# Delta rule on one Trainium2 core: three groups of 64x64 products written as tiles of 64 rows by 32 columns

## The reference

```python
def rwkv7_scan(r, w, k, v, kk, a, S0):
    def step(S, xs):
        r_t, w_t, k_t, v_t, kk_t, a_t = xs
        sa = jnp.einsum('bhvk,bhk->bhv', S, -kk_t)
        S = (S * w_t[:, :, None, :] + sa[..., None] * (kk_t * a_t)[:, :, None, :]
             + v_t[..., None] * k_t[:, :, None, :])
        y = jnp.einsum('bhvk,bhk->bhv', S, r_t)
        return S, y
```

## Time and profile before

| | |
|---|---|
| Median of 3 runs | 2491.67 us (2488.76 to 2494.94) |
| Profiled execution | 2489.43 us, span 2487.6 us |
| TensorE busy | 2423.0 us, 97% of the span, 46610 matmul records |
| VectorE, ScalarE busy | 1280.5 us (51%), 606.9 us (24%) |
| DMA | 500.52 MB, mean 201 GB/s |
| RWKV block of layer 0 | from about 395 to 670 us |
| RWKV block of layer 1 | from about 1385 to 1656 us |

### The profile page before, as it was taken

How to read it: one execution, slowest core, us unless ns; L and a number is a source line. 1 busy time by engine, 2 the same in 40 slices (tenths; PEclk the granted TensorE clock), 3 DMA queues, 4 the chain that set the end, 5 groups by cost and what they waited for, 6 DMA issues and landing times. The chain is left out here.

```text
span 2487.6 us, 105448 instructions
## 1 busy us (share of the span) xinstructions
PE 2423.0 (97%) x46610; PEld 2013.6 (81%) x46610; DVE 1280.5 (51%) x3333; ACT 606.9 (24%) x1798; POOL 0.2 (0%) x4
## 2 busy tenths in 40 slices
PE   9999999999999999999999999999999999999998
PEld 7987666666699999898766666679899989888887
DVE  7666666666687676756665666668311111111111
ACT  2234333433311100223333334321111111111111
POOL 0000000000000000000000000000000000000000
PEclk9999999999999999999999999999999999999999
DMA  6334432222243443333343222234799999999997
GB/s 251 129 138 146 165 121 88 84 84 80 101 154 133 157 165 138 133 134 137 137 162 129 82 77 84 84 105 152 300 363 397 383 371 407 400 381 408 387 392 309
DMA packets 146068, 500.52 MB, mean 201 GB/s; under 512 B 18784, under 2 KB 23520, under 8 KB 143360
## 3 DMA queue, kind: packets, MB, share of 16 engines
q1 hardware_dynamic: 145792, 496.44, 53.5%
HBM read 476.08 MB, written 20.29 MB: 200 GB/s over the span
## 5 line engine op out<-in xcount | busy, mean ns | idle before, releaser
L302 PE MATMUL psum<-hT,ring 128*64 128x144 f32 (+1 forms) x4568 | 458.5, 346 | 3.4 <-DVE hT L2430 1.7
L455 PE MATMUL psum<-work,ring 128*64 128x88 f32 (+3 forms) x11264 | 417.6, 232 | 16.2 <-issue 5.8
L455 PEld LDWEIGHTS psum<-work,ring 128*64 128x64 f32 x11264 | 399.3, 136 | 35.4 <-issue 30.1
L302 PEld LDWEIGHTS psum<-hT,ring 128*64 128x64 f32 x4568 | 294.4, 137 | 95.0 <-issue 11.3
L2966 DVE TENSOR_TENSOR work<-psum,work 128x88 f32<-128x88 f32 (+3 forms) x176 | 42.4, 241 | 362.7 <-PE psum L455 362.5
L2667 PE MATMUL psum<-work,proj 128*64 128x88 f32 (+3 forms) x5632 | 203.5, 232 | 6.1 <-issue 4.5
L2667 PEld LDWEIGHTS psum<-work,proj 128*64 128x64 f32 x5632 | 196.8, 136 | 12.6 <-issue 9.6
L1776 ACT ACTIVATE work<-psum 128x256 f32<-128x256 f32 (+4 forms) x320 | 103.9, 362 | 349.9 <-PE psum L1687 84.8
L302 PE MATMUL psum<-work 128*64 128x144 f32 (+4 forms) x2096 | 155.4, 283 | 4.3 <-DVE work L1267 3.6
L302 PE MATMUL psum<-y_ret,work 128*64 128x144 f32 x2400 | 156.2, 286 | 0.8 <-DVE y_ret L532 0.8
L302 PEld LDWEIGHTS psum<-y_ret,work 128*64 128x64 f32 x2400 | 148.6, 137 | 1.0 <-issue 1.0
(11 more groups left out here) (518 smaller groups left out, 3695.7 us busy)
## 6 DMA issues: line engine op xcount, KB each, us to landing
ring<-w_ff_dram SPq DMA_DIRECT2D x424, 512.0 KB, 7.4
ring<-w_mix_dram SPq DMA_DIRECT2D x256, 512.0 KB, 3.8
proj<-w_ff_dram SPq DMA_DIRECT2D x128, 512.0 KB, 5.5
proj<-w_ff_dram SPq DMA_DIRECT2D x64, 384.0 KB, 5.8
work<-s_gla_dram SPq DMA_DIRECT2D x8, 1024.0 KB, 4.9
gla_s_out<-work SPq DMA_DIRECT2D x8, 1024.0 KB, 4.7
work<-s_ret_dram SPq DMA_DIRECT2D x8, 512.0 KB, 5.1
ret_s_out<-work SPq DMA_DIRECT2D x8, 512.0 KB, 2.7
```

The lines of the kernel that those rows point to most:

```text
L302: last = nc.tensor.matmul(out[64 * c:64 * c + 64], weights[:, 64 * c:64 * c + 64], x, start=start, stop=stop)
L455: mm = nc.tensor.matmul(out[64 * c:64 * c + 64], ring[:, s, k, 64 * c:64 * c + 64], rhs[:, k0 + k, :], start=(k0 + k == 0), stop=(k0 + k = ...
```

## The change

Three groups of products in the RWKV block are written with a new helper, `in_quarters`: the first product of every level (`level_w`), the product of the last level, and keys by values in `right_side`. The two halves of a pair are cut in two each, at 32 columns of the stationary operand, so that for each c four matmuls on tiles of 64 rows by 32 columns stand in place of two on 64 by 64. The order for a c is: columns 0 to 31 of both halves, then columns 32 to 63 of both. Each of the four streams all 64 columns of its half's moving operand. Results, waits and semaphores stay as they were. Operands, buffers and all other instructions too.

```diff
+            def in_quarters(outs, weights, xs):
+
+                for j in range(0, CH, 32):
+                    for r in range(2):
+                        last = mm(outs[r][j:j + 32], weights[r][:, j:j + 32], xs[r], start=True, stop=True)
+                return last
+
             def level_w(i, n):
...
                 for c in range(6 if n == 0 else 4):
-                    for r in range(2):
-                        last = mm(unit(half(W, r), c), half(AT, 1 - r)[:, c], half(X, 1 - r)[:, c], start=True, stop=True)
+                    last = in_quarters([unit(half(W, r), c) for r in range(2)], [half(AT, 1 - r)[:, c] for r in range(2)],
+                                       [half(X, 1 - r)[:, c] for r in range(2)])
                 last.then_inc(sig("W1_ps"), 1)
...
                 else:
                     for c in range(4):
-                        for r in range(2):
-                            last = mm(unit(half(W, r), 4 + c), half(W1, r)[:, c], half(XT, r)[:, c], start=True, stop=True)
+                        last = in_quarters([unit(half(W, r), 4 + c) for r in range(2)],
+                                           [half(W1, r)[:, c] for r in range(2)], [half(XT, r)[:, c] for r in range(2)])
...
                 for c in range(4):
-                    for r in range(2):
-                        mm(unit(half(W, r), c), half(PkPr, r)[:, c, 0], half(vtok, r)[:, c], start=True, stop=True)
+                    in_quarters([unit(half(W, r), c) for r in range(2)], [half(PkPr, r)[:, c, 0] for r in range(2)],
+                                [half(vtok, r)[:, c] for r in range(2)])
```

## The result

The changed kernel takes 2498.88 us (median of 14 runs, 2495.83 to 2500.73), the kernel before in the same session 2490.95. The ratio is 1.0029, 95% interval 1.0021 to 1.0037, that is 5.2 to 9.2 us slower. The forecast was 2498 by a sum of +6.4 us.

The account below looks back on a forecast made before the run. TensorE's instruction stream, busy 97%, was taken as the bound. Slabs 0 to 6 at +0.42 us each (14 of them, 5.9) plus 0.5 for the last slabs gave +6.4 us on 2491.67: 2498, range 2491 to 2504.

Parts of the forecast that it names:

- Rounds: Changed bursts: a round of four 64x32 tiles takes about 0.056 us instead of 0.058; a plain 8-round burst 0.03 us less.
- (c): Changed bursts: two column tiles over the same 64 rows take turns, rounds of 0.11 us, +53 us, 2545; chance 3%.
- (d): Changed bursts: four tiles do a pair's work in half the rounds, -27 us plus 9.5 of size changes, 2474; chance 3%.
- (b): Changed bursts: rounds no quicker than 0.058 us, or new waits; 8 to 11 us slower, 2500 to 2503; chance 18%.
- Size changes: Where 64x32 meets another tile size: the stream plus about 0.095 us, 0.15 after 64 columns, 0.34 after 288.
- rival (a): Between 64x64 and 64x32 tiles: no drain, so bursts keep their overlap; -3 us, 2489; chance 8%.
- levels 0 to 3: First products between 128-row filler, size changes already paid: -0.04 and three times -0.03, -0.13 us a slab.
- Level 4 as a whole: Slabs 0 to 6: first product leaves the key norm's shadow, +0.34 us; second product before the bonus sum, -0.065.
- Right side: Sample products, keys by values, states to filler: two size changes break a seamless run, 1.31 to 1.59 us, +0.28 a slab.
- The last slabs: Last slab of each layer, without norm or bonus sum: +0.25 us, twice, 0.5; its last product loses overlap, +0.13.
- the filler's 14 waits for ScalarE: Filler behind level 4's first product: waits averaging 0.18 us, 2.5 in all, vanish as the burst ends later.
- ScalarE's chain: Level 4's product, table load and norm's root start 0.4 us later but have slack; no cost, if binding up to 1.4 us.

Follow-up runs that it names:

- the early key values: Kernel before with only the state's 64x64 key values moved from behind the bonus sum to behind level 4's first product: 2488.78 us against 2490.66, ratio 0.9991.

## Why the prediction was right

**Rounds.** Right to the third digit: a burst of 8 rounds spans 0.435 us between its first and last record (0.463 before), one of 12 rounds 0.658. The first gap is 0.080 and the later rounds are (0.435 - 0.080 - 0.020)/6 = 0.056 us, which is the stream of 64 columns as the prediction worked it out. Rivals (c) and (d), and the slower round of (b), needed another round, and none was seen.

**Size changes.** Right: 0.145 to 0.149 us from the last record of one size to the first of the other where 64 columns streamed, at 64x64 to 64x32 as at 64 to 128 rows, and 0.333 behind the norm's 288 columns. The weakest evidence of the prediction was one place with 32 columns behind it; it held, and rival (a) fell at the same places. The Trainium skill's rule that a change of tiling mode drains while a change of tile doesn't ("TensorEngine Tiling (Array Packing)", section "Key Properties") agrees with the runs, also between two modes of the same row size: 0.14 us a slab came back with one size change less, 0.25 with the norm in the burst's size.

**The sum.** Per slab: levels 0 to 3 forecast -0.13, alone -0.135. Level 4 as a whole forecast +0.34 - 0.065 = +0.275; in the changed kernel 0.33 - 0.08 = +0.25 to +0.26. Right side forecast +0.28, measured +0.27. Together +0.42 forecast, +0.405 measured. The last slabs +0.25 forecast, +0.23 measured where no stop falls in; the last product's part, +0.13, was 0.12 alone. Both blocks: 6.4 forecast, 6.1 by these distances. That the profile has 6.5 is in part luck: it holds the two stops of 0.24 us, which no term of the sum stood for.

**The waits.** That the filler's 14 waits for ScalarE would vanish, and that ScalarE's chain would have slack, were both right: in the blocks no wait of TensorE for another engine grew. The stops wait for nothing that the profile shows.

**What was not foreseen.** The time rose by 7.9 us between the medians and 7.2 by the ratio, the blocks by 6.5. The difference is inside the interval. The forecast of 2498 also stood on a median for the kernel before, 2491.67, that is 0.7 us above the 2490.95 measured beside the changed kernel; without that help it would have been 2497.4 for 2498.9 measured. By their ratios nearly all kernels of the study lie 0.5 to 2 us above what their slabs account for (the two with level 4's first product or the last product alone don't), those that gained as well as those that lost. Each of these differences is inside its interval. The stops are a part of them, 0.5 us in the changed kernel and 0.8 in the one with levels 0 to 3 alone, each in one profiled execution; the rest stays open. As to the class, I gave 0.57 to a change within 0.3% and 0.39 to one above. The ratio came out at 0.29%, on the edge, as the sum had it.

## What to carry to other kernels

Before cutting a product into smaller tiles ask what a round of it pays for: if it is the streaming of columns, smaller stationary tiles save at most the difference to the load, and the idle half of the array stays idle, since where operands and results lie decides which tiles can be used. Count the neighbours: a burst between instructions of another size pays its drain already, but one that runs seamlessly beside or behind its neighbours loses the drain, the hidden load and the overlap. And a wait that a loss has silently used up is a place for other work: here it was worth 0.23 us a slab, the tiles of levels 0 to 3 0.135.

## What the runs showed of the hardware

Dense bursts of small instructions stop now and then with nothing to wait for. In the kernel with levels 0 to 3 in 64x32 tiles and the early key values, the level 0 burst of slab 2 (counted from 0, in layer 0) stops before its last 8 load records, for 0.23 us. TensorE's weight loads there:

```profile
471.10 0.29 PEld L1570 LDWEIGHTS psum<-work 64*32 64x32 f32 x16
471.63 0.16 PEld L1570 LDWEIGHTS psum<-work 64*32 64x32 f32 x8 [0.23 <-issue]
```

The same burst stops in slab 6 too, and is whole in the other slabs of layer 0. It cost 0.28 and 0.29 us in these two, and 0.16 in one slab of layer 1. The kernel without the early key values has 0.15 and 0.16 in the same two slabs and 0.49 in one of layer 1, the run with the norm in quarters and the rest as before 0.11 in one slab, and the changed kernel the two stops of 0.24 that are shown with the result. The run with the norm in the same tiles has one of 0.24 in the last slab of layer 0. The run with the sample products in quarters too lost most, 1.9 us in all, 1.2 of it in one slab, where the profile has 0.8 us of "issue" ahead of L1696. Not only the new tiles are hit: the first of the changed kernel's two stops is in a burst of 64x64 tiles, and the version with the four in another order has it at the same place. The kernel before has none in its RWKV blocks, nor have the runs with one of the other three products alone, nor that with the early key values alone; so all that stop have levels 0 to 3 in the new tiles. Since the matmuls of such a burst are twice as many in the same time, it would fit that the engine runs out of instructions, but that wasn't tested, nor why it falls on some slabs. Against a gain of 0.03 us a burst a stop is large, so it alone can undo a good part of the tiles' gain.
